# A tile-wise norm at the start, an overflow loop of three rounds of five, and a copy moved ahead of an add, in a two-block transformer kernel on one core

## What is computed

```python
def rms_norm(x, g):
    xf = xf * lax.rsqrt(jnp.mean(xf * xf, axis=-1, keepdims=True) + NORM_EPS)
...
xn = rms_norm(h, norm1_g[l])
proj = xn @ w_in[l]                      # q, k, v, qi, ki, wi, su, sv, ga, gb
q = rope(q, positions) ...               # rotary angles from the positions
...
# hierarchical experts: each token goes to 2 of 32 experts
hdn = lax.ragged_dot(xs, w_e_in, group_sizes)
act = jax.nn.silu(gate_h) * up_h
ys = lax.ragged_dot(act, w_e_out, group_sizes)
jnp.zeros_like(xt).at[tok_sorted].add(ys)
```

## Time and profile before

| | |
|---|---|
| median of 3 runs | 1778.15 us (1776.95 to 1781.03) |
| the profiled execution, its own time | 1777.38 us |
| its span in the profile | 1775.4 us |
| mean granted TensorE clock | 0.958 |
| stage one of the experts | about 596 to 837 us |
| stage two of the experts | about 1287 to 1756 us |

### The profile page before, as it was taken

The page is one execution under the profiler, slowest core; times in us unless marked ns, Lnnn a source line. Parts: engine busy times, 40 slices in busy tenths (PEclk is TensorE's granted clock), DMA queues, the critical chain, the costliest instruction groups (busy, mean ns, idle before and its releaser), DMA issues.

```text
span 1775.4 us, 19376 instructions
## 1 busy us (share of the span) xinstructions
PE 1601.1 (90%) x7674; PEld 1029.8 (58%) x7674; DVE 818.0 (46%) x1351; ACT 357.9 (20%) x591; POOL 237.8 (13%) x295
## 2 busy tenths in 40 slices
PE   5999999999999696977799979998699997999996
PEld 4688888877888342323688857777533332333333
DVE  6798745537374410112732358974433232323233
ACT  3322100027101110101311176561201010010101
POOL 0100003300000310111200024762120000000000
PEclk9999999999999898999799988999899998999998
DMA  4222222220337999998332200005899999999993
GB/s 161 86 95 95 72 95 95 96 81 15 112 125 299 321 401 428 428 427 342 141 119 71 95 1 0 1 8 220 324 351 429 431 430 426 406 431 428 432 429 136
DMA packets 52774, 403.17 MB, mean 227 GB/s; under 512 B 13632, under 2 KB 14912, under 8 KB 23504
## 3 DMA queue, kind: packets, MB, share of 16 engines
q1 hardware_dynamic: 45264, 389.34, 54.7%
q0 software_dynamic: 7424, 12.61, 2.0%
HBM read 397.69 MB, written 16.81 MB: 233 GB/s over the span
## 4 chain that ended last, share of the span: by engine, by line
PE 76%; DMA 8%; DVE 6%; issue 4%; ACT 3%; POOL 2%; SPq 0%; POOLq 0%; DVEq 0%; ACTq 0%
PE bank L1677 38%; PE bank L710 17%; PE bank L725 8%; DMA arena<-in_expert_in 6%; PE bank L689 3%; DMA arena<-in_expert_out 2%; PE bank L1669 1%; PE bank L690 1%; PE bank L1780 1%; PE bank L1829 1%; PE bank L1911 1%; PE bank L1796 1%; PE bank L1903 1%; PE bank L1954 1%; DVE resid L1082 1%
## 5 line engine op out<-in xcount | busy, mean ns | idle before, releaser
L710 PE MATMUL bank<-arena 128*64 128x512 f32 x960 | 277.1, 621 | 29.6 <-issue 10.7
L710 PE MATMUL bank<-ring,arena 128*64 128x512 f32 x576 | 181.1, 608 | 10.4 <-issue 8.8
L710 PEld LDWEIGHTS bank<-arena 128*64 128x64 f32 x960 | 84.4, 142 | 177.2 <-issue 174.7
L1082 DVE TENSOR_TENSOR resid<-resid,bank 128x512 f32<-128x512 f32 x120 | 81.8, 685 | 208.4 <-PE bank L690 208.4
L2327 DVE CAST ring_high<-ring 128x2048 fp32r<-128x2048 f32 x53 | 65.1, 1228 | 242.6 <-DMA ring<-in_stream_a 146.9
L2328 DVE TENSOR_TENSOR ring_low<-ring,ring_high 128x2048 fp32r<-128x2048 f32 x60 | 138.7, 2312 | 6.2 <-ACT ring_high L2038 4.2
L725 PE MATMUL bank<-arena 128*64 128x512 f32 x448 | 114.4, 595 | 8.2 <-issue 5.3
L1677 PE MATMUL bank<-ring_low,xn_high 128*128 128x512 f32 x288 | 112.9, 392 | 0.0
L1677 PE MATMUL bank<-ring_high,xn_high 128*128 128x512 f32 x288 | 112.1, 389 | 0.0
L1677 PE MATMUL bank<-ring_high,xn_low 128*128 128x512 f32 x288 | 112.1, 389 | 0.0
L710 PEld LDWEIGHTS bank<-ring,arena 128*64 128x64 f32 x576 | 55.3, 139 | 69.0 <-issue 68.9
(11 more groups left out here) (384 smaller groups left out, 3020.0 us busy)
## 6 DMA issues: line engine op xcount, KB each, us to landing
ring<-in_stream_a SPq DMA_DIRECT2D x42, 1024.0 KB, 5.0
arena<-in_expert_gate SPq DMA_DIRECT2D x20, 2048.0 KB, 14.9
arena<-in_expert_in SPq DMA_DIRECT2D x18, 2048.0 KB, 26.8
arena<-in_expert_up SPq DMA_DIRECT2D x18, 2048.0 KB, 18.1
arena<-in_expert_down SPq DMA_DIRECT2D x18, 2048.0 KB, 19.1
ring<-in_expert_up SPq DMA_DIRECT2D x12, 2048.0 KB, 18.4
ring<-in_expert_down SPq DMA_DIRECT2D x12, 2048.0 KB, 17.0
ring<-in_expert_gate SPq DMA_DIRECT2D x12, 2048.0 KB, 17.2
```

The lines of the kernel that those rows point to most:

```text
L710: last = nc.tensor.matmul(h[side * SLOTS:(side + 1) * SLOTS, :], tokens[:, k, side * SLOTS:(side + 1) * SLOTS], w[:, k * 512:(k + 1) * 512 ...
L1082: nc.vector.tensor_tensor(place, place, bank[bank_at][:, :], ALU.add).then_inc(m.moe_added, 1)
```

## The change

**Start.** The table of constants is put in another order and loaded in two parts: the first 240 columns (unit matrix, inverse frequencies, the exponent of the root) ahead of x, the rest behind the first streamed piece. POOL makes the root of each tile as soon as that tile is summed. DVE computes the angles of one function, then scales all four tiles, one wait each; the other function's angles come after the split of the first piece. PE turns tile by tile into all eight banks, and its `kiwi` product waits unit by unit. The high parts of the first two streamed pieces go to ACT.

```diff
-HIGH_BY_ACT = range(7, 14)
+HIGH_BY_ACT = (0, 1, *range(7, 14))
...
+            sp.dma_start(cst[:, 0:EARLY_CONSTANTS], consts_in[:, 0:EARLY_CONSTANTS]).then_inc(consts_in_s, 16)
             for t in range(NT):
                 sp.dma_start(x[:, t, :], x_in[t * P:(t + 1) * P, :]).then_inc(x_in_s[t], 16)
-                if t == 0:
-                    sp.dma_start(cst[:, :], consts_in).then_inc(consts_in_s, 16)
...
+                if n == 0:
+                    sp.dma_start(cst[:, EARLY_CONSTANTS:], consts_in[:, EARLY_CONSTANTS:]).then_inc(consts_rest, 16)
...
-            pe.wait_ge(scaled, NT)
-            for k in range(KC):
-                transposes(("xT", k), [xs[:, t, k * P:(k + 1) * P] for t in range(NT)])
+            turned = [begin(("xT", k)) for k in range(KC)]
+            for t in range(NT):
+                pe.wait_ge(scaled, t + 1)
+                for k in range(KC):
+                    last = nc.tensor.transpose(turned[k][:, t * P:(t + 1) * P], xs[:, t, k * P:(k + 1) * P], c("ident"))
...
+            for k in range(KC):
+                wait_read(pe, ("xT", k))
+                for i, (w_, x_) in enumerate(((0, 1), (1, 0), (0, 0))):
+                    last = nc.tensor.matmul(b[0:72, :], kiwi_parts[w_][:, k, :], xn_parts[x_][:, k, :],
...
+            angles(0, 0.25)
+            for t in range(NT):
+                dve.wait_ge(rms, t + 1)
+                V.tensor_scalar(xs[:, t, :], x[:, t, :], rstd[:, t:t + 1], None, ALU.mult).then_inc(scaled, 1)
...
+            split_weights(1)
+            angles(1, 0.0)
             split_weights(2)
```

```diff
-            n_over = pe.value_load(m.over[0:1, 0:1], min_val=0, max_val=OVER)
-            with pe.Fori(0, OVER) as v:
-                with pe.If(v < n_over):
+            n_over = pe.value_load(m.over[0:1, 0:1], min_val=0, max_val=OVER_GROUPS)
+            with pe.Fori(0, OVER_GROUPS) as group:
+                with pe.If(group < n_over):
+                    for one in range(OVER_AT_ONCE):
...
-                V.tensor_copy(m.over[:, 0:1], upto_[:, NE - 1:NE]).then_inc(routed, 1)
+                groups = tmp(1)
+                then(V.tensor_scalar(groups, upto_[:, NE - 1:NE], 0.0, None, ALU.is_gt))
+                for n in range(1, OVER_GROUPS):
+                    then(V.scalar_tensor_tensor(groups, upto_[:, NE - 1:NE], float(n * OVER_AT_ONCE), groups,
+                                                ALU.is_gt, ALU.add))
+                V.tensor_copy(m.over[:, 0:1], groups).then_inc(routed, 1)
```

```diff
-                if m.b == 1 and 1 <= p < PAIRS - 1:
-                    add_dve(dve, m, p - 1, 2 * NT - 2, COMBINE_BANK)
                 dve.wait_ge(m.at_done, p + 1)
                 V.tensor_copy(m.actT[:, 0:m.F, :].rearrange("p f s -> p (f s)"), bank[4][:, 0:m.width])\
                     .then_inc(m.actT_ready, 1)
+                if m.b == 1 and 1 <= p < PAIRS - 1:
+                    add_dve(dve, m, p - 1, 2 * NT - 2, COMBINE_BANK)
...
+                def last_spread_unit(p=p):
+
+                    pe.wait_ge(m.moe_added, units_before(p - 1) + 2 * NT - 2)
+                    pe.wait_ge(m.xgT_act, p + 2)
+                    spread_pe(pe, m, p - 1, 2 * NT - 1, LAST_UNIT_BANK)
```

More of the change, by code:

```diff
@@ L65, in constant_table @@
     put("ident", (row == col) * 1.0)
+    put("invf", 10000.0 ** (-np.arange(0, HD, 2, dtype=np.float32) / np.float32(HD))[None, :])
+    put("nhalf", np.full((1, 48), -0.5))
     put("ones", np.ones((P, P)))
@@ L781, in over_sp @@
             sp.wait_ge(routed, 2 * m.b + 2)
[L782 to L793, removed]
+            n_over = sp.value_load(m.over[0:1, 0:1], min_val=0, max_val=OVER_GROUPS)
+            with sp.Fori(0, OVER_GROUPS) as group:
+                with sp.If(group < n_over):
+                    for one in range(OVER_AT_ONCE):
+                        for i in range(len(m.sources)):
+                            m.wait_used(sp, m.over_at + i - MOE_SLOTS)
+                        e = sp.value_load(m.over[0:1, bass.ds(group * OVER_AT_ONCE + (one + 1), 1)], min_val=0, max_val=NE - 1)
+                        for i, source in enumerate(m.sources):
+                            width = HALF_TILE if m.parts == 1 and i == 1 else TILE
+                            src = source[bass.ds(e, 1), :, :].rearrange("e p c -> p (e c)")
+                            sp.dma_start(m.over_slots[i][:, 0:width], src).then_inc(m.over_tile[i], 16)
+                        sp.wait_ge(m.over_stored if m.b == 0 else m.over_added, group * (16 * OVER_AT_ONCE) + 16 * one + 16)
+                        alone(sp)
         def moe_source(m, n, half):
@@ L955, in over_act @@
             A = nc.scalar
[L956 to L971, removed]
+            n_over = act.value_load(m.over[0:1, 0:1], min_val=0, max_val=OVER_GROUPS)
@@ L2002, in _ @@
                     .then_inc(sumsq, 1)
-            act.wait_ge(rms, 1)
-            act.wait_ge(sumsq, NT)
-            for t in range(0, NT, 2):
-                nc.scalar.activation(xs[:, t, :], x[:, t, :], ACT.Copy, scale=rstd[:, t:t + 1]).then_inc(scaled, 1)
             act.wait_ge(small_in, 32)
@@ L2009, in _ @@
                 b = unit(("xT", k))
-                if k == 0:
-                    act.wait_ge(scaled, NT)
                 nc.scalar.activation(xn_parts[0][:, k, :], b[:, :], ACT.Copy, scale=g1[:, k:k + 1])\
                     .then_inc(high_ready, 1)
+            high_part(0)
+            b = unit("kiwiT")
+            read(nc.scalar.copy(kiwiT, b[0:72, :]))
+            high_part(1)
             act.wait_ge(angles_ready, 2)
@@ L2018, in _ @@
                 .then_inc(trig_ready, 1)
-            b = unit("kiwiT")
-            read(nc.scalar.copy(kiwiT, b[0:72, :]))
             b = unit("kiT")
@@ L2341, in _, with angles @@
             magic = 1.5 * 2.0 ** 23
-            for j, quarter in ((0, 0.25), (1, 0.0)):
+            def angles(j, quarter):
                 r = trig[:, j, :]
@@ L2356, in _ @@
             V.tensor_tensor(lo, kv_, hi.bitcast(F32), ALU.subtract).then_inc(kiwi_split, 1)
-            dve.wait_ge(rms, 1)
-            dve.wait_ge(sumsq, NT)
-            for t in range(1, NT, 2):
-                V.tensor_scalar(xs[:, t, :], x[:, t, :], rstd[:, t:t + 1], None, ALU.mult).then_inc(scaled, 1)
-            dve.wait_ge(scaled, NT)
             for k in range(KC):
@@ L2787, in _ @@
             pool.wait_ge(consts_in_s, 16)
+            for t in range(NT):
+                inverse_rms(pool, t, TILES_BEFORE["in"] + t + 1, then)
+            pool.wait_ge(consts_rest, 16)
             G.tensor_copy(count_ones[:, 0, :], c("tri_lt")).then_inc(ids_ready, 1)
-            pool.wait_ge(sumsq, NT)
-            then(G.tensor_scalar(rstd[:, 0:4], ssq[:, 0:4], 1.0 / D, EPS, ALU.mult, ALU.add))
-            G.tensor_tensor(rstd[:, 0:4], rstd[:, 0:4], c("nhalf")[:, 0:4], ALU.pow).then_inc(rms, 1)
             rotations = 0
```

308 lines of the change are left out of this document (166 added, 142 removed).

## The result

Before, the median of 9 executions is 1777.72 us (1776.44 to 1781.50); with the change it is 1767.48 us (1760.53 to 1772.38, 9 executions). The ratio is 0.9936, 95% interval 0.9923 to 0.9949: faster by 0.64%, about 11 us (10.2 by the two medians). The sum had said 16. The time lies in the stated range of 1757 to 1770, but outside the forecast's own range of 1758 to 1766. The profiled execution of the changed kernel is one of its longer ones: its own time is 1771.49, its span 1769.8, 5.6 less than the 1775.4 before.

A forecast was written before the change was run, and what follows sets the result against it. PE was taken to bound the kernel (76% of the chain of waits). Start 6.8 plus stage two 9.2, capped by tiles, made 16.0 off 1777.4: 1761.4, as median 1762 us; own range 1758 to 1766, stated range 1757 to 1770.

The forecast's parts named there:

- The start: Kernel start: constants split and x scaled earlier, so `qi` starts at 23.6 instead of 30.42, 6.8 us gained.
- the cap by the tiles: Late stage two: from about pair 10 PE waits about 1 us a pair for tiles, so its own 16.3 isn't reached.
- the copy: Stage two, activations to down product: copy without the add ahead starts 0.33 us earlier, 4.7 us over fourteen pairs.
- the start's gain being lost: Rival: start's gain lost at a later place going by DMA, leaving 9.2 alone, 1769 us; chance 0.08.
- fetches on DVE: Stage two: only DVE's loop fetches at each branch, about 1769 us; a part of rival 1.
- The loop: PE's skipped loop in stage two: twelve rounds fewer, pause 10.65 to 1.65 us; with full clock PE could gain 11.6.
- rival 1: Stage two: each of the loop's six branches fetches its target, about 5 us more, 1772 us; chance 0.17.
- full clock after: Stage two, behind PE's shortened pause of 1.65 us: the restart runs at full clock, worth 2.6 us more.
- Where the three meet: End of stage two: tile stream limits PE, so the end comes 9.2 us forward, not PE's own 16.3.
- What the stream regains: Stage two, 1500 to 1530 us: stream at 395 instead of 429 GB/s for want of free places, 2.4 us to regain.
- The lag of 7.2: Pair 15 of stage two: PE takes the second up tile 7.2 us after landing, a lead the change would recover.
- Stage one gives nothing: Stage one: DMA share is 1.00 and a fixed tile stream sets its end, so the shorter loop gains nothing.

The follow-up runs named there:

- e2: Only the start's edits on the kernel before: median 1771.12 us, ratio 0.9960.
- e11: Changed kernel with its skipped loop as one round of fifteen instead of three of five: 1767.57 us, one execution.
- e1: The changed kernel run again unaltered, 6 executions: median 1764.47 us, ratio 0.9927 to the kernel before.
- e12: Changed kernel with its skipped loop as five rounds of three instead of three of five: 1771.07 us, one execution.

## Why the prediction came out as it did

The start, the cap by the tiles and the copy came as forecast in kind; the sum was too large by 3 to 6 us. That 1767.48 lies in the stated range is in part luck: its upper part, above 1766, was there for the start's gain being lost and for fetches on DVE, and neither is what made the time. The order of the two main terms also came out turned round: 6.8 and 9.2 were forecast for start and stage two, 6.7 and 5.6 measured.

**The start: right.** 6.8 forecast, 6.5 in the profile at `qi`, 6.7 in the median of e2. Two sizes in it were off and cancelled: the constants landed at 4.95 instead of 4.1, and the last tile's root came at 13.65 instead of 12.2, so DVE's low parts began 0.6 late; but eight of them took 5.36 us and not the 5.90 of before, and they ended at 21.1, where the forecast had 21.0.

**The loop: mechanism right, size wrong.** One branch in six fetches, as forecast against rival 1. The fetch was sized by the old row of 3.04, but a jump over five blocks takes 5.8 to 6.4. So the pause was 4.27 to 4.85 instead of 1.65. With a pause that long, "full clock after" failed as well: the clock fell within it, at 1487.56, and from gate to up pair 7 took 11.71 us. Only in e11, after a pause of 2.75, did it stay (9.31 from gate to up). PE thus gained 5.9 here, not 11.6.
The Trainium skill, "Runtime: NRT & Kernel Launch", section "Instruction fetch mechanics", says that an engine's instruction store is only two lines of 16 KiB (256 instructions each) and that a taken branch out of them forces a fetch; it also gives PE 128 KiB. The changed kernel's body in stage two has 340 matmuls and as many weight loads, and behind one branch of 6363 ns the two other jumps over it took 221 each: this goes against a fetch at each such branch on PE. How much PE really holds no run here shows.

**The copy: right.** A pair takes 28.58 us (the gate products of pairs 9 and 10 start at 1549.10 and 1577.68) instead of 28.93: 0.35 each, 0.33 forecast. Alone it is worth 3.6 (by the ratio) to 4.5 (by the medians).

**Where the three meet: right in kind, and here is the step that failed.** Forecast was 9.2 = 7.2 + 2.4 - 0.4. The lag of 7.2 was there: 6.96 before, 0.13 after, 6.8 given back. "What the stream regains", 2.4, was not: the last up tile landed 445.9 us after the stage's start before and 445.4 after, so 0.5. The dip to 395 GB/s in the earlier trace rows was real in bytes, but the eight tiles landing across it took 39.95 us before (1503.78 to 1543.73) and 39.63 after (1503.66 to 1543.29). Counted over the last 48 tiles up to pair 15's last up tile, the stream takes 238.5 us before and 238.0 in the changed kernel; e2, whose dip is deeper (313 GB/s from 1500 to 1510), takes 240.8. So a dip does cost time, but this one cost 0.5 and not 2.4. Where the other missing bytes went, no run looked into. And a loss was missing, the 1.7 of half clock behind the wait of 2.60. So 6.8 + 0.5 - 1.7 = 5.6, which is the measured difference of the two stages. Waits began at pair 12 instead of 10, since the pause had been sized too small; in e11, with a pause of 2.75 and full clock behind it, they began at pair 10. They took 0.6 us a pair and not about 1, as tiles came every 29.2 us a pair and not every 29.9.

**Stage one gives nothing: right**, with 242.1 us against 240.9. The seven profiles with a loop of three rounds have 239.5 to 242.1 and those of the old loop 239.0 to 240.9; whether its change costs up to 1 us there stays open.

**The sum.** 6.7 + 5.6 is 12.3, against 13.4 (e1) and 10.2 (the first nine) by the medians and 11.1 by the mean spans (1775.4 over all 54 executions of before, less 1764.3). What the remaining 1 us is wasn't settled; with executions 12 us apart it can't be told from chance.

## What to carry to other kernels

When several edits speed up one engine of a stage that another resource feeds, cost them together: the most that they can give is the lag of the engine behind the feed at the stage's end, and an edit that comes near it leaves little for the others. How much time a dip of the transfer rate costs is read from the landings of the items behind it, not from the missing bytes. When an engine has caught up, its idle time comes back as waits for the feed, here above all as one at the end; put work there that has to be done anyway, so that the clock stays up too.

## What the runs showed of the hardware

- A hardware loop whose rounds are all skipped has at most one long branch on PE, its first. In stage two (68 matmuls a block) it takes 2.6 to 3.0 us with a body of one block and 5.8 to 6.4 with three, five or fifteen. In stage one (22 matmuls a block) it takes up to 0.25 with one block, 0.37 to 0.47 with three or five, and 6.1 with fifteen. All later skip branches are 0.21 to 0.23. So the size of the body alone doesn't decide; what does stays open.
- In each long branch a 16 KB block on the instruction queue begins 2.3 to 2.5 us before its end (fifteen of fifteen).
- The clock falls after pauses of the same length in one execution and not in the next: behind the pause of 2.46 us near 1145 it fell in eleven of fourteen profiles, and behind the wait of 2.6 us at pair 15 in four (up product 8.6 to 8.8 us) and not in e12 (7.10). Executions of the changed kernel lie 12 us apart, and over 43 executions of the kernel before the span falls by 0.7 us for each 0.001 of mean granted clock (0.951 to 0.961). That the falls make the spread is thus likely, not shown.
